# A two-way RWKV-7 scan on four quarters of TensorE's array, with its level matrices on GpSimd and its inverse blocks read two chunks ahead

## What is computed

```
def step(S, inp):
    r_t, w_t, k_t, v_t, a_t, b_t = inp
    sa = jnp.einsum('bhij,bhj->bhi', S, a_t)
    S = (S * w_t[:, :, None, :] + sa[..., :, None] * b_t[..., None, :]
         + v_t[..., :, None] * k_t[..., None, :])
    return S, jnp.einsum('bhij,bhj->bhi', S, r_t)
```

## Time and profile before

| | us |
|---|---|
| median of three runs | 2507.27 |
| the profiled execution, its time | 2509.72 |
| its span, first to last instruction | 2508.0 |
| scan, from the first `level_n` of body 0 | 792.5 to 1181.0 |
| its first DMA issues | 752.8 |
| TensorE busy over the span | 2328.4 (93%) |
| VectorE, ScalarE, GpSimd busy | 1827.3, 1208.3, 709.5 |

### The profile page before, as it was taken

How to read it: one execution, slowest core, us unless ns; L and a number is a source line. 1 busy time by engine, 2 the same in 40 slices (tenths; PEclk the granted TensorE clock), 3 DMA queues, 4 the chain that set the end, 5 groups by cost and what they waited for, 6 DMA issues and landing times. The chain is left out here.

```text
span 2508.0 us, 50080 instructions
## 1 busy us (share of the span) xinstructions
PE 2328.4 (93%) x19504; PEld 2035.2 (81%) x19504; DVE 1827.3 (73%) x2480; ACT 1208.3 (48%) x1748; POOL 709.5 (28%) x715
## 2 busy tenths in 40 slices
PE   6899999999996999996989896699999999999997
PEld 4788888888876898986767674699999999999996
DVE  5547888988865676675767677677777777777777
ACT  6355454445522334432335332566565666666656
POOL 2234242433412444454453534011011111101111
PEclk9999999999997999998999998799999999999998
DMA  4335253442537766763647352777777777777777
GB/s 151 85 96 162 86 161 116 137 149 87 172 114 226 210 188 188 192 173 79 234 128 258 111 202 101 301 246 256 264 256 245 237 258 255 251 251 260 264 256 245
DMA packets 294772, 479.74 MB, mean 191 GB/s; under 512 B 142224, under 2 KB 209952, under 8 KB 266832
## 3 DMA queue, kind: packets, MB, share of 16 engines
q1 hardware_dynamic: 275552, 412.52, 50.1%
q0 software_dynamic: 7760, 27.08, 4.8%
q10 hardware_dynamic: 11296, 37.82, 4.6%
HBM read 363.51 MB, written 110.69 MB: 189 GB/s over the span
## 5 line engine op out<-in xcount | busy, mean ns | idle before, releaser
L2751 PE MATMUL bank<-e_xt,e_w_high 128*128 128x384 f32 x1792 | 524.7, 357 | 3.7 <-DVE e_xt L2919 2.1
L2906 DVE TENSOR_TENSOR e_w_low<-e_w,e_w_high 128x2048 fp32r<-128x2048 f32 x192 | 436.2, 2284 | 69.2 <-ACT e_w_high L2807 69.2
L2752 PE MATMUL bank<-e_xt,e_w_low 128*128 128x192 f32 x1792 | 449.1, 251 | 0.0
L2807 ACT ACTIVATE e_w_high<-e_w 128x2048 fp32r<-128x2048 f32 x192 | 366.4, 1908 | 107.8 <-PE bank L2773 79.2
L2752 PEld LDWEIGHTS bank<-e_xt,e_w_low 128*128 128x128 f32 x1792 | 342.2, 191 | 0.6
L2751 PEld LDWEIGHTS bank<-e_xt,e_w_high 128*128 128x128 f32 x1792 | 338.1, 189 | 5.5 <-issue 2.5
L462 PE MATMUL bank<-h_high,w_high 128*128 128x512 f32 x864 | 258.0, 407 | 1.5 <-DVE work L872 1.5
L855 DVE SCALAR_TENSOR_TENSOR work<-work,vec 128x1551 f32<-128x1551 f32 x116 | 243.8, 2102 | 2.4
L465 PE MATMUL bank<-h_low,w_high 128*128 128x512 f32 x864 | 244.8, 391 | 0.0
L468 PE MATMUL bank<-h_high,w_low 128*128 128x512 f32 x864 | 243.7, 390 | 0.0
L2685 POOL DMA_INDIRECT xacc_dram<-e_y,e_put x30 | 47.3, 1576 | 651.9 <-DVE e_y L2941 647.3
(11 more groups left out here) (356 smaller groups left out, 5168.7 us busy)
## 6 DMA issues: line engine op xcount, KB each, us to landing
e_w<-in_ew SPq DMA_DIRECT2D x192, 1024.0 KB, 5.9
features_dram<-work SPq DMA_DIRECT2D x48, 512.0 KB, 3.3
fe<-features_dram SPq DMA_DIRECT2D x24, 1024.0 KB, 8.1
x_w<-in_w_mix SPq DMA_DIRECT2D x48, 512.0 KB, 5.1
w<-in_w_in ACTq DMA_DIRECT2D x35, 512.0 KB, 3.6
ba_tok_dram<-work SPq DMA_DIRECT2D x96, 128.0 KB, 2.2
gates_dram<-work ACTq DMA_DIRECT2D x16, 768.0 KB, 4.5
all<-ba_tok_dram SPq DMA_DIRECT2D x96, 128.0 KB, 3.4
```

What stands on the lines that cost most here:

```text
L2751: nc.tensor.matmul(*wide, start=(k == 0), stop=False)
L2752: nc.tensor.matmul(*narrow, start=False, stop=False)
L2807: nc.scalar.activation(w_high[n % RING][:], w[n % RING][:], ACT.Copy).then_inc(w_high_done, 1)
L2906: tt(w_low[n % RING][:], w[n % RING][:], w_high[n % RING][:].bitcast(F32), ALU.subtract)\
```

## The change

- Direction 1 uses the other two quarters: rows 0-63 with columns 64-127, and rows 64-127 with columns 0-63. `level_n`, `level_x`, `solve` and the products run both directions interleaved in one group. Where direction 1's results must change halves, ScalarE copies half by half (`swapped`).
- The products are grouped anew: `products_wide` (128 columns, with G) five chunks ahead (`FIRST`), `products_narrow` and `products_c` four ahead. The ring `ALL` has six slots (`RING_ALL`).
- `state(i-2)` stands first in body i; it was `state(i-1)` at the end.
- `levels` moves from VectorE to GpSimd, four operations on the blocks that aren't zero. The norm of the convolution moves to GpSimd too, its squares to ScalarE.
- SyncE's order: `diagonal`, `features` and `inverses` (both at even i), `tokens`, `compact(i+2)`, `keys`, `lower(i+5)`. `compact` for direction 1 is three DMAs. `values` moves to ScalarE's queue, as do direction 1's first `lower`, `diagonal` and `compact`. At the start, `features(1)` waits for the landing of `features(0)`. The last pair is no longer inverted in two halves.

```diff
-LEVELS, AHEAD, RING = 2, 4, 5
+LEVELS, AHEAD, FIRST, RING, RING_ALL, PARTS = 2, 4, 5, 5, 6, 3
...
-ALL = many("all", [P, HP, 5, CH], RING)
-B_, A_, M_, G_, RB_ = range(5)
+ALL = many("all", [P, HP, 5, CH], RING_ALL)
+B_, A_, M_, G_, RB_ = (0, 2), (1, 1), (2, 0), (3, 3), (4, 4)
...
+STATE, TOKEN = ROWS, ROWS[::-1]
+HALF = [ROWS, ROWS[::-1]]
...
+def compact(eng, d, i):
+    m = i // 2
+    eng.wait_ge(x_out[m % 2], 16 * (m // 2 + 1))
...
+    if d == 0:
+        eng.dma_start(XC[d][i % 2][:].rearrange("p h x c -> p h (x c)"), src).then_inc(l_x[d][i % 2], 16)
+    else:
+        eng.dma_start(XC[d][i % 2][:, :, 0, :], src[:, :, 0:BASE]).then_inc(l_x[d][i % 2], 16)
+        for out, r in zip(ROWS, HALF[d]):
+            eng.dma_start(XC[d][i % 2][out, :, 1, :], src[r, :, BASE:2 * BASE]).then_inc(l_x[d][i % 2], 16)
...
-def values(i):
...
+def inverses(m):
+    inverted(sp, m)
+    sp.dma_start(g.x_dram[m, :, :], XB[m % 2][:].rearrange("p r x c -> p (r x c)")).then_inc(x_out[m % 2], 16)
...
 features(0)
+for d in DIRS:
+    featured(sp, d, 0)
 features(1)
 for i in range(2):
+    lower(sp, 0, i)
+for i in range(2):
+    diagonal(sp, 0, i)
+features(2)
+tokens(0)
+lower(sp, 0, 2)
+inverses(0)
+lower(sp, 1, 2)
+for i in range(2):
+    compact(sp, 0, i)
+for d in DIRS:
+    lower(sp, d, 3)
+for i in (2, 3):
     for d in DIRS:
-        lower(d, i)
-diagonal(0)
-diagonal(1)
-features(2)
-for d in DIRS:
-    lower(d, 2)
-tokens(0)
-inverses(0)
+        diagonal(sp, d, i)
 keys(0)
-values(0)
-compact(0)
-compact(1)
-for d in DIRS:
-    lower(d, 3)
-diagonal(2)
-diagonal(3)
 features(3)
 tokens(1)
 keys(1)
-values(1)
...
 for i in range(NCH):
     if i == 0:
         for d in DIRS:
-            lower(d, AHEAD)
-        inverses(1)
-        compact(2)
-    if 1 <= i and i + AHEAD - 1 < NCH:
-        diagonal(i + AHEAD - 1)
-    if i % 2 == 1 and 3 <= i < NCH - 3:
-        inverses((i + 1) // 2)
-    if i % 2 == 0 and i >= 4:
-        compact(i + 1)
+            lower(sp, d, FIRST - 1)
+    if i + FIRST - 1 < NCH:
+        for d in DIRS:
+            diagonal(sp, d, i + FIRST - 1)
+    if i % 2 == 0 and 2 <= i < NCH - AHEAD - 2:
+        features((i + AHEAD + 2) // 2)
+    if i % 2 == 0 and i < NCH - 2:
+        inverses((i + 2) // 2)
     if 1 <= i < NCH - 1:
         tokens(i + 1)
-    if i % 2 == 0 and 2 <= i < NCH - AHEAD - 2:
-        features((i + AHEAD + 2) // 2)
-    if i % 2 == 1 and i >= 3 and i + 1 < NCH:
-        compact(i + 1)
-    if i == 1:
-        compact(3)
+    if i + 2 < NCH:
+        for d in DIRS:
+            compact(sp, d, i + 2)
     if 1 <= i < NCH - 1:
         keys(i + 1)
-    if 1 <= i < NCH - AHEAD:
+    if i + FIRST < NCH:
         for d in DIRS:
-            lower(d, i + AHEAD)
-    if 1 <= i < NCH - 1:
-        values(i + 1)
+            lower(sp, d, i + FIRST)
     if i == 2:
         sp.dma_start(cv[:], g.conv_dram[:, :, MIX_ORDER[0] * BLK:(MIX_ORDER[0] + 1) * BLK]).then_inc(c_in, 16)
-    if i in (NCH - 4, NCH - 3):
-        inverses(N_PAIRS - 1, i - NCH + 4)
...
     for hp in L4:
-        for r in ROWS:
-            mm = nc.tensor.matmul(t_bank(d)[r, hp, :], NL[d][s][r, n, hp, :], x[d][s][r, hp, 0, :],
-                                  start=True, stop=True)
-    mm.then_inc(m_n[d], 1)
...
+        for d in DIRS:
+            for z, r in enumerate(ROWS):
+                mm = nc.tensor.matmul(t_bank(d)[HALF[d][z], hp, :], NL[d][s][r, n, hp, :],
+                                      x[d][s][r, hp, 0, :], start=True, stop=True)
+            if hp == HP - 1:
+                mm.then_inc(m_n[d], 1)
...
+        for y in range(2) if n < LEVELS - 1 else (None,):
+            for d in DIRS:
+                side = d if y is None else y
+                for r, own in zip(ROWS, HALF[d]):
+                    pair = (x[d][s][own, hp, 1, :], T1[d][own, hp, :])
+                    left, right = pair if side == 0 else pair[::-1]
+                    mm = nc.tensor.matmul(x_bank(d)[r, hp, side, :], left, right, start=True, stop=True)
+                if hp == HP - 1 and y != 0:
...
+    for hp in L4:
+        for d in DIRS:
+            for z, r in enumerate(ROWS):
+                mm = nc.tensor.matmul(bank[EARLY[d]][HALF[d][z], hp * P:(hp + 1) * P],
+                                      XX[d][i % 2][r, hp, d, :],
+                                      ALL[d][i % RING_ALL][r, hp, B_[d]:RB_[d] + 1:RB_[d] - B_[d], :],
                                       start=True, stop=True)
...
+def products_wide(j):
...
+    for hp in L4:
+        for d in DIRS:
+            c = inner(d, j)
+            for z, r in enumerate(ROWS):
+                ar, kb = AR[d][u][r, hp, :, c], KB[d][u][r, hp, :, c]
+                left, right = (kb[:, 1, :], ar) if d == 0 else (ar[:, 0, :], kb)
+                mm = nc.tensor.matmul(wide_of(d, j)[HALF[d][z], hp, :], left, right, start=True, stop=True)
+            if hp == HP - 1:
+                mm.then_inc(m_w[d], 1)
+def products_narrow(j):
...
     post, pre = i >= 1, i + AHEAD < NCH
-    for d in DIRS:
-        level_n(d, i, 0)
+    if i >= 2:
+        for d in DIRS:
+            state(d, i - 2)
+    level_n(i, 0)
     if post:
-        for d in DIRS:
-            solve(d, i - 1)
-    for d in DIRS:
-        level_x(d, i, 0)
+        solve(i - 1)
+    level_x(i, 0)
+    if pre:
+        products_narrow(i + AHEAD)
     if post:
         full(0, i - 1)
-    if pre:
-        products(0, i + AHEAD)
-    for d in DIRS:
-        level_n(d, i, 1)
+    if i + FIRST < NCH:
+        products_wide(i + FIRST)
+    level_n(i, 1)
     if post:
         full(1, i - 1)
     if pre:
-        products(1, i + AHEAD)
+        products_c(i + AHEAD)
+    level_x(i, 1)
+def conv_sum(i, ready, value, done):
+    pe.wait_ge(ready, value)
     for d in DIRS:
-        level_x(d, i, 1)
-    if post:
-        state(0, i - 1)
-    if pre:
-        products_c(i + AHEAD)
-    if post:
-        state(1, i - 1)
...
+    for out, src in swapped(d):
+        ins = copy(GH[d][out, :, :].rearrange("p h c -> p (h c)"), bank[EARLY[d]][src, :])
+    ins.then_inc(a_g[d], 1)
+def swapped(d):
+    return ((slice(0, P), slice(0, P)),) if d == 0 else tuple(zip(ROWS, ROWS[::-1]))
...
+    if n == 0 and i >= 2:
+        act.wait_ge(m_g[d], i - 1)
+    for out, src in swapped(d) if n == 0 and side == 1 else swapped(0):
+        ins = copy(XX[d][i % 2][out, :, side, :], x_bank(d)[src, :, side, :])
...
+    if i >= 2:
+        for d in DIRS:
+            out(d, i - 2)
     if i >= 1:
         for d in DIRS:
             solved(d, i - 1)
-    for n in range(LEVELS):
+    for side in range(2):
         for d in DIRS:
-            level_x(d, i, n)
+            level_x(d, i, 0, side)
+    if i >= 2:
+        for d in DIRS:
+            store(d, i - 2)
+            values(d, i)
+    if i + AHEAD < NCH:
+        for d in DIRS:
+            receptance(d, i + AHEAD)
     for d in DIRS:
-        if i + AHEAD < NCH:
-            receptance(d, i + AHEAD)
-        if i >= 1:
-            out(d, i - 1)
-            store(d, i - 1)
-    if i == 9:
+        level_x(d, i, 1, d)
...
+def levels(d, i):
+    if i >= 2:
+        pool.wait_ge(m_n[d], (i - 1) * LEVELS)
+    pool.wait_ge(v_g[d], i + 1)
+    for n, blocks in enumerate((slice(1, None, 2), slice(2, None))):
+        part = lambda v: v.rearrange("p h (b c) -> p h b c", c=BASE)[:, :, blocks, :]
+        level = mk("level", n * HD, HD).unsqueeze(1).to_broadcast([P, HP, HD])
+        ins = tt(part(NL[d][i % 2][:, n, :, :]), part(ALL[d][i % RING_ALL][:, :, G_[d], :]), part(level),
+                 ALU.mult)
+    ins.then_inc(p_n[d], 1)
...
+def conv(i):
+    add = lambda out, a, b: tt(out[:], a, b, ALU.add)
+    if i == 4:
+        pool.wait_ge(c_in, 16)
+        ch.count(add(ya[0], cv[:, 0, :], cv[:, 1, :]))
+        ch.link(add(ya[1], cv[:, 2, :], cv[:, 3, :]))
+        add(ya[0], ya[0][:], ya[1][:]).then_inc(c_added, 1)
...
 invert(1)
 for i in range(1, NCH - 1):
     for d in DIRS:
+        levels(d, i + 1)
+    for d in DIRS:
         expand(d, i + 1)
-    if i % 2 == 0 and i + 4 < NCH:
-        invert((i + 2) // 2)
-    if i in (19, 20):
-        for d in DIRS:
-            pool.wait_ge(p_x[d], i + 2)
-        invert(N_PAIRS - 1, i - 19)
-        pool.wait_ge(p_c, N_PAIRS - 1 + i - 19)
+    if i % 2 == 1 and i + 3 < NCH:
+        invert((i + 3) // 2)
+    conv(i)
     if i == 21:
         pool.wait_ge(ln_in, 32)
         for q in range(QT):
...
 @block.vector
...
     post, pre = i >= 1, i + AHEAD < NCH
-    level_n(0, i, 0)
-    if i in (5, 9):
+    level_n(i, 0)
+    if i in (6, 12):
         conv_read(i)
-    level_n(1, i, 0)
-    if i + 1 < NCH:
-        levels(0, i + 1)
+    if i >= 2:
+        for d in DIRS:
+            carried(d, i - 2)
+    if pre:
+        for d in DIRS:
+            masked_narrow(d, i + AHEAD)
     aside(i)
     if post:
         summed(0, i - 1)
-    if pre:
-        masked(0, i + AHEAD)
-    for d in DIRS:
-        level_n(d, i, 1)
-    if i + 1 < NCH:
```

(46 more changed lines are left out.)

453 lines of the change are left out of this document (208 added, 245 removed).

## The result

The changed kernel takes 2544.6 us (median of four runs, 2540.3 to 2548.2) against 2507.2 for the kernel before on the same chip: ratio 1.0147, 95% interval 1.0126 to 1.0169. It is slower by 37 us. The forecast was 2469 us, with a chance of 0.09 for slower.

The account below looks back on a forecast made before the run. TensorE was taken to bound the middle of the scan before, SyncE's in-order queue after. Gains of 18 us in bodies 2 to 17, 3 at the start and 17 at the end, together 38, gave 2469 us from 2507.3; range 2430 to 2494.

Parts of the forecast that it names:

- Part 1: TensorE in a scan body: four quarters, 64-column records at 22 ns, so it needs 11.1 us (9.6 to 14.8).
- Part 2: Other engines per body: VectorE 9.2 us, ScalarE about 10.2, GpSimd 8.8, none over 11.1; chain across engines 12 to 13.5.
- B: Rival in the scan: SyncE's stall is hidden and engines bind at about 13 us a body; 2437 us, chance 0.27.
- Part 3: SyncE's in-order queue as new bound: compact waits for inverse blocks behind features, 29.8 us a pair, 14.9 a body.
- longest landing: Case of SyncE's loop: inverse blocks land 9.8 us behind their issue, 32 us a pair, 16.0 a body.
- the forecast's 238: Time forecast for bodies 2 to 17 of the scan, in us, at 14.9 us a body.
- A: Leading case in the scan: SyncE's loop binds, 14.0 to 15.4 us a body; 2455 to 2484, forecast 2469, chance 0.43.
- The ends: Start and end of the scan: 3 us gained at the start, 17 at the end (87 against 104.2).
- the 11 and the 24 are estimates: End of the scan: one body of 11 us and a drain of 24, estimated from the last bodies of before.
- E: Rival, no change: a pair of bodies costs 34.5 us by a longer landing, the ends give their 20 back; chance 0.04.
- C: Rival on TensorE: four quarters give nothing, records stay at 30.6 ns, 15.3 us a body; 2478 us, chance 0.17.
- D: Rival on TensorE's clock: idle pieces halve it; slower from a half-clock share of 0.56, 2533 us at 0.7; chance 0.09.

Follow-up runs that it names:

- e10: The changed kernel with features issued at the end of the odd body and the even body's compact behind lower; 2521.9 us, ratio 1.0062.
- e12: The changed kernel with features late, even-body compact behind lower, VectorE's centring late in bodies 19 and 20, keys issued by ScalarE; 2519.0 us, ratio 1.0047.
- e1: The changed kernel with the inverse blocks issued ahead of the features in even bodies; 2537.3 us, ratio 1.0125.
- e2: The changed kernel with features moved from the even body to the end of the odd one, behind lower; 2528.1 us, ratio 1.0087.
- e9: The changed kernel with SyncE's compact of the even body issued behind keys and lower; 2523.2 us, ratio 1.0061.
- e11: The changed kernel with features late, even-body compact behind lower, and VectorE's centring of y late in bodies 19 and 20; 2513.8 us, ratio 1.0032.
- e8: The changed kernel with VectorE's centring of y in bodies 19 and 20 moved to the end of the body; 2538.8 us, ratio 1.0144.
- e6: The changed kernel with features at the end of the odd body, tokens ahead of diagonal, and ScalarE's receptance late; 2540.5 us, ratio 1.0137.

## Why the prediction was wrong

**Part 1, four quarters: right in the rate, wrong in what was left out.** I took 22 ns for a 64-column record and it was 15.6 to 17; the 128-column ones start 27 ns apart (32 from 927.43, the last at 928.27), near my 28. By these a body is 128 x 17 + 96 x 15.6 ns, 64 x 27, and 2.2 twice: 9.8 us against my 11.1. The step that failed is the sum "TensorE then needs 11.1 us a body": it prices the stream alone. The same number of instructions has to be supplied in less time, and the stops take 43 us in 16 bodies, 2.7 each, and up to 3.8 once SyncE's waits are gone. The trace of the kernel before had the sign of it: 9 stops, 8.7 us, at the ends of such blocks, in "issue" waits of up to 1.8 us that I read as nothing.

**Part 2, the other engines: nearly right.** GpSimd's level operation was taken at 0.47 us:

```profile
L1594 POOL TENSOR_TENSOR nl<-all,masks 128x128 f32<-128x128 f32 x41 | 17.5, 463 | 0.0
```

VectorE has 8.8 us a body (I had 9.2), ScalarE 8.1 busy besides its issues, GpSimd 9.2. None binds. With SyncE's waits gone the bodies of e10 and e12 still took 16.3 and 16.1 us, so B's 13 us was out of reach.

**Part 3, SyncE's loop: the mechanism as written, mis-sized.** A pair of bodies took 276.8 / 8 = 34.6 us, not 29.8. Count from the end T of `lower`'s issues in the even body. In the rows above T is 960.29: the second `diagonal` of the odd body is out at T+2.0 (2.9), the odd body ends at T+13.0 (12.0), features at T+15.9 (15.9), and the inverses go out at 976.29, T+16.0 (17.0). That pair is the quickest; the mean over the eight is T+17.6, so up to there it holds within 0.6 us. From the issue of the inverses to the next T it is 16.9 us in the mean (15.9 to 18.0) instead of 12.8. The inverse blocks take 9.0 us to land in the mean (8.0 to 9.9; 942.65 to 952.26 in the rows), where T+17.0 and T+23.3 make 6.3; the rest is issue time, in the rows 2.1 us for the keys instead of 1.1 and 3.6 for `lower` instead of 2.9. That is the term that failed: 4.1 us a pair, 33 us in eight pairs of the 39 between 238 and 277. My own "longest landing" case, 9.8 behind the issue, was nearly the true one. I gave it 16.0 a body; its own terms (17.0, 9.8, 2.2, 1.1, 2.9 and 0.3) make 33.3 us, 16.6 a body, and 1.4 us more of issue time a pair bring it close to what was measured. e1 and e2 show that the landing behind features is only 7 to 16 us of the time; e9 shows that its place ahead of keys and `lower`, and so ahead of the next inversion, is 21. But the two causes aren't additive: with the loop cut, e10 stays at 16.3 us a body, and nearly all of TensorE's idle time there is late code. So with the loop cut the bodies still take 22 us more than the forecast's 238, and together with the lost ends (below) that keeps e10, e11 and e12 over the range. What the loop alone costs isn't shown, since every version with four quarters has late blocks.

Three smaller slips of the sums: A's 15.4 us a body gives 2477, not 2484; the second `diagonal`, out at T+2.9 with 2.4 to land, lands at T+5.3, not T+4.9; and at the end 27 us were counted and 26 added. None of them decides the outcome.

**The ends.** I had 3 us of gain at the start and 17 at the end; they became losses of 2.6 and 12.7. At the end the failed step is "the 11 and the 24 are estimates": bodies 18 to 22 were counted as bound by the inversion alone. In the trace TensorE waits 12.5 us in one piece for VectorE's `fu`, which stands behind the centring, which waits 7.9 us for y loads that SyncE issues late. e8 puts 6 us on this. Why the start is later I did not test; body 0 begins 4.1 us later already (796.6 for 792.5).

**The rivals.** A's mechanism with E's size: the pair cost 34.6 us, E's 34.5 "by a longer landing", but the ends gave nothing back, and so it was slower. C, that four quarters give nothing, is refuted by the records. D, the clock, is partly there: 0.89 over bodies 2 to 17 is a bit over a fifth of the time at 1.2 GHz, far from D's threshold of 0.56. TensorE was busy 12.2 us a body for work that takes 9.8 at full clock, so at most 2.4 us a body; how much of it was on the path stays open, since no run held the clock up. It moves little, 0.89 in the changed kernel and 0.92 in e11, while the time changes by 31 us.

## What to carry to other kernels

A kernel that needs less TensorE time for the same number of instructions asks for its code sooner: count instructions per unit of time, and when "issue" stops inside a group are spaced evenly in instruction count, compare their ends with the packets of the instruction queue. When a stage's pace is a loop through a queue in order, write the loop down from one issue to its next instance and move everything out of it that doesn't feed the next round; the longest wait in the table need not be in it. And before giving a range, take the landing of a transfer behind bulk data in the same queue at its worst row, together with the worst issue times.

## What the runs showed of the hardware

- Four 64x64 quarters in turn sustain one f32 record of 64 columns in 15.6 ns (64 records in 1.00 us), where two took 30.6.
- TensorE's code comes in 16 KB packets of 256 instructions. At each of the 30 stops in bodies 2 to 17 of the changed kernel TensorE goes on 1.2 to 2.1 us after a packet's end, and the longest stop is 4.8 us.
- A record of an f32 matmul with 128x128 weights and 64 columns starts every 112 ns; two on the column halves, 128x64 each, take 60 ns together.
- A DMA issue on SyncE took 0.3 to 1.1 us in most cases (median 0.6 in bodies 2 to 17 of the changed kernel), 2.5 us at 979.83 in e6 and 3.9 us at 895.24 in e10. With 18 a body, SyncE of e10 was issuing for 235.4 of 260.5 us.
- The 256 KB of inverse blocks landed 8.0 to 9.9 us after their issue behind 2 MB of features, and 3.6 to 4.8 us in bodies 0, 18 and 20, which load none.
